# Rotary embedding in a two-layer diffusion backbone: the rotated half taken by transfers within SBUF instead of a TensorE product

## The reference, cut to what matters

```python
def apply_rope(x, cos, sin):
    q = HEAD_DIM // 4                      # 16 of the 64 rows of a head
    x0, x1, x2, x3 = x[..., :q], x[..., q:2 * q], x[..., 2 * q:3 * q], x[..., 3 * q:]
    rot = jnp.concatenate([-x1, x0, -x3, x2], axis=-1)
    return x * cos + rot * sin
```

## Time and profile before

| | |
|---|---|
| median of 3 runs | 1598.11 us (1596.82 to 1600.96) |
| the profiled execution, its own time | 1596.81 us |
| its span | 1594.7 us |
| PE busy, DVE busy | 1553.0 us (97%), 789.8 us (50%) |
| granted TensorE clock | 0.998 over the span |
| line 1970, rotation products | 28 records: two for each of 14 tiles |
| weights, SP line 532 | 180 transfers of 512 KB, median 3.5 us to landing |

### The profile page before, as it was taken

The page is one execution under the profiler, slowest core; times in us unless marked ns, Lnnn a source line. Parts: engine busy times, 40 slices in busy tenths (PEclk is TensorE's granted clock), DMA queues, the critical chain, the costliest instruction groups (busy, mean ns, idle before and its releaser), DMA issues.

```text
span 1594.7 us, 25334 instructions
## 1 busy us (share of the span) xinstructions
PE 1553.0 (97%) x10785; PEld 1290.1 (81%) x10785; DVE 789.8 (50%) x1276; ACT 550.1 (34%) x725; POOL 541.4 (34%) x244
## 2 busy tenths in 40 slices
PE   6999999899999999999999999999999999999998
PEld 3888754478888888888888888855479998998997
DVE  5897786678466534333234333666534221221324
ACT  5744335464322112221122234255544322222233
POOL 0040046413323332332233223256643444444442
PEclk9999999999999999999999999999999999999999
DMA  9532100052233333333433222200022222223223
GB/s 376 209 119 67 54 28 0 3 205 101 93 132 132 110 129 133 119 119 139 150 110 131 66 69 73 72 14 1 1 67 93 93 93 93 93 93 106 94 93 106
DMA packets 44607, 158.55 MB, mean 99 GB/s; under 512 B 4784, under 2 KB 8240, under 8 KB 42960
## 3 DMA queue, kind: packets, MB, share of 16 engines
q1 hardware_dynamic: 44064, 156.74, 28.1%
q0 software_dynamic: 432, 0.20, 0.1%
HBM read 154.95 MB, written 2.10 MB: 98 GB/s over the span
## 4 chain that ended last, share of the span: by engine, by line
PE 75%; DVE 2%; ACT 1%; issue 1%; POOL 1%; DVEq 0%; POOLq 0%
PE psum L1850 67%; PE psum L2099 2%; PE psum L1927 1%; PE psum L2067 1%; DVE osb L1379 1%; PE psum L1998 1%; PE psum L1895 1%; POOL acc L622 1%; PE psum L2115 0%; DVE mx L1275 0%; PE psum L2084 0%; PE psum L2073 0%; PE psum L2071 0%; PE psum L2069 0%; PE psum L1970 0%
## 5 line engine op out<-in xcount | busy, mean ns | idle before, releaser
L1850 PE MATMUL psum<-act,whi 128*128 128x258 f32 (+2 forms) x3968 | 784.5, 318 | 0.0
L649 POOL TENSOR_TENSOR wlo<-raw,whi 128x1024 fp32r<-128x1024 f32 (+1 forms) x162 | 390.4, 2410 | 791.2 <-ACT whi L683 791.2
L1850 PEld LDWEIGHTS psum<-act,whi 128*128 128x128 f32 x3968 | 588.1, 189 | 57.3 <-issue 3.7
L1850 PE MATMUL psum<-act,wlo 128*128 128x512 f32 (+1 forms) x1984 | 472.1, 316 | 0.0
L1850 PEld LDWEIGHTS psum<-act,wlo 128*128 128x128 f32 x1984 | 309.0, 189 | 26.7
L683 ACT ACTIVATE whi<-raw 128x1024 fp32r<-128x1024 f32 (+1 forms) x180 | 187.1, 1040 | 336.2 <-DMA raw<-weights_dram 336.1
L1176 DVE SCALAR_TENSOR_TENSOR tmps<-psum,rs 128x256 f32<-128x256 f32 (+1 forms) x176 | 78.2, 486 | 349.1 <-PE psum L1850 345.6
L1128 DVE SCALAR_TENSOR_TENSOR product<-adr,cb 128x1024 f32<-128x1024 f32 x128 | 177.6, 1418 | 5.9 <-ACT cb L750 3.0
L1619 DVE SCALAR_TENSOR_TENSOR xT<-psum,mod,xT 128x512 f32<-128x512 f32 x93 | 58.3, 655 | 223.6 <-PE psum L1850 223.6
L1850 PE MATMUL psum<-gh,whi 128*128 128x512 f32 x507 | 152.6, 357 | 0.0
L1850 PE MATMUL psum<-gh,wlo 128*128 128x512 f32 x507 | 152.5, 358 | 0.0
(11 more groups left out here) (205 smaller groups left out, 1313.0 us busy)
## 6 DMA issues: line engine op xcount, KB each, us to landing
raw<-weights_dram SPq DMA_DIRECT2D x180, 512.0 KB, 3.5
adr<-adat_dram SPq DMA_DIRECT2D x80, 512.0 KB, 4.7
ada_w<-ada_dram SPq DMA_DIRECT2D x8, 1024.0 KB, 14.3
xT<-x_in_dram SPq DMA_DIRECT2D x3, 1024.0 KB, 16.9
xT<-x_in_dram SPq DMA_DIRECT2D x2, 1536.0 KB, 8.0
cb<-crow_dram SPq DMA_DIRECT2D x2, 1024.0 KB, 10.6
out_dram<-fin SPq DMA_DIRECT2D x8, 256.0 KB, 2.3
stage<-weights_dram SPq DMA_DIRECT2D x1, 512.0 KB, 9.4
```

The costliest lines, as they stand in the source:

```text
L649: nc.gpsimd.tensor_tensor(wlo[:, s, 0:w], raw[:, s, 0:w], whi[:, s, 0:w].bitcast(F32), ALU.subtract).then_inc(sem("s_lo"), 1)
L1850: last = MM(out_[:, o:o + t1 - t0], w_, a_[:, t0:t1], start=k == order[0] and j == 0, stop=k == order[-1] and j == 2)
```

## The change: what it does

`rotated` and its matrix `rot` are gone from PE's program, with the waits on `a_nrm`, `a_rsin` and layer 1's `s_tile` that stood beside it. In its place SP issues eight transfers for each of the 14 tiles (`turn`): 16 partitions of 512 f32 (32 KB) each, from the head tile into `ropet`, quarter q taken from quarter q XOR 1. `ropet` is then multiplied by the sine in place. The negation moves into the table of the sine. SP waits for `a_nrm` (layer 0) or `s_tile` (layer 1), and for an earlier `a_rope`, so that the buffer is free. DVE waits for all eight transfers of a tile. In DVE's program only layer 1's last block changes its order.

```diff
+        TURNED = {11: (0, 0), 13: (0, 1), 14: (0, 2), 16: (0, 3), 17: (0, 4)}
+        TURNED.update({FIRST[("proj", 1)] + (j + 2 if j else 1): (1, j) for j in range(9)})
...
+        def turned(L, j):
+            return sem(f"a_rot{j % 2}"), 16 * 8 * (j // 2 + 1 + L * (3 - j % 2))
...
+            def turn(L, j):
+                if L == 0:
+                    sp.wait_ge(sem("a_nrm"), j + 1)
+                    if j >= 1:
+                        sp.wait_ge(sem("a_rope"), j)
+                else:
+                    sp.wait_ge(sem("s_tile"), 19 + (j + 2 if j else 1))
+                    if j >= 2:
+                        sp.wait_ge(*na("rope", 1, j - 1))
+                src_, dst_ = prep_tiles(L)[j][0], rope_place(L, j)
+                for q in range(8):
+                    a, b = 16 * q, 16 * (q ^ 1)
+                    sp.dma_start(dst_[a:a + 16, :], src_[b:b + 16, 0:NX]).then_inc(turned(L, j)[0], 16)
...
+                if n - RING + 1 in TURNED:
+                    turn(*TURNED[n - RING + 1])
...
             def roped_sine(L, j):
-                dve.wait_ge(*na("rot", L, j + 1))
-                if L == 0 and j >= 1:
-                    dve.wait_ge(sem("a_rope"), j)
-                TT(ropet[L][:, j % 2 * L, 0:NX], rot_out(L, j), sin, ALU.mult).then_inc(sem("a_rsin"), 1)
+                dve.wait_ge(*turned(L, j))
+                TT(rope_place(L, j), rope_place(L, j), sin, ALU.mult).then_inc(sem("a_rsin"), 1)
...
                     if b["m"] == 9:
-                        roped_sine(1, 7)
                         maxima(1, 1, 4)
-                        roped_sine(1, 8)
                         top(1, 1)
-                        roped(1, 7, sine=False)
-                        roped(1, 8, sine=False)
+                        roped(1, 7)
+                        roped(1, 8)
...
-            def rotated(L, j):
-                if L == 0:
-                    pe.wait_ge(sem("a_nrm"), j + 1)
-                elif j >= 2:
-                    pe.wait_ge(*na("rsin", L, j - 1))
-                MM(rot_out(L, j), rot, prep_tiles(L)[j][0][:, 0:NX], start=True, stop=True) \
-                    .then_inc(sem("a_rot"), 1)
...
-    con[:, CC_SIN:CC_SIN + NX] = np.tile(np.sin(ang), (2, 1))
+    con[:, CC_SIN:CC_SIN + NX] = np.tile(np.sin(ang), (2, 1)) * np.where(np.arange(P) % (2 * quarter) < quarter, -1.0, 1.0)[:, None]
...
-    con[:, CC_ROT:CC_ROT + P] = np.kron(np.eye(2), r)
```

More of the change, by code:

```diff
@@ L75 @@
 CC_BLK = CC_ONES + P
-CC_ROT = CC_BLK + P
-CC_MF = CC_ROT + P
+CC_MF = CC_BLK + P
 CC_MB = CC_MF + CH
@@ L344, in build @@
         blk = con[:, CC_BLK:CC_BLK + P]
-        rot = con[:, CC_ROT:CC_ROT + P]
         cos = con[:, CC_COS:CC_COS + NX]
@@ L363, in build @@
         names += [f"s_{n}" for n in ("sq", "sqadd", "nps", "rs", "nhh", "nhl")]
-        names += [f"a_{n}" for n in ("sq", "ms", "rs", "nrm", "rot", "rsin", "rcos", "rope", "khi", "klo", "zone", "vps",
+        names += [f"a_{n}" for n in ("sq", "ms", "rs", "nrm", "rot0", "rot1", "rsin", "rcos", "rope", "khi", "klo", "zone", "vps",
                                      "vtok", "qhi", "qlo", "M", "mx", "top", "R", "neg", "e", "S", "exp", "add", "pv", "sum",
@@ L391, in build @@
         ALL = {"m": sum(len(u["pieces"]) for u in U[0]), "t": sum(len(u["steps"]) for u in U[0])}
-        ONCE = {"rot": 5, "rsin": 5, "rcos": 5, "rope": 5, "khi": 1, "klo": 1, "vps": 1, "vtok": 1, "qhi": 4, "qlo": 4,
+        ONCE = {"rsin": 5, "rcos": 5, "rope": 5, "khi": 1, "klo": 1, "vps": 1, "vtok": 1, "qhi": 4, "qlo": 4,
                 "M": ALL["m"], "mx": ALL["m"], "S": ALL["t"], "exp": ALL["t"], "pv": ALL["t"],
@@ L462, in prep_tiles, with rope_place @@
                 [(ksrc(1), None)] + [(bigs[1][:, 2 + t, :], None) for t in range(8)]
[L464 to L468, removed]
+        def rope_place(L, j):
+            return ropet[L][:, j % 2 * L, 0:NX]
+        def turned(L, j):
+            return sem(f"a_rot{j % 2}"), 16 * 8 * (j // 2 + 1 + L * (3 - j % 2))
         def vT_out(L):
@@ L1226, in roped_sine, with roped @@
             def roped_sine(L, j):
-                dve.wait_ge(*na("rot", L, j + 1))
-                if L == 0 and j >= 1:
-                    dve.wait_ge(sem("a_rope"), j)
-                TT(ropet[L][:, j % 2 * L, 0:NX], rot_out(L, j), sin, ALU.mult).then_inc(sem("a_rsin"), 1)
-            def roped(L, j, sine=True):
+                dve.wait_ge(*turned(L, j))
+                TT(rope_place(L, j), rope_place(L, j), sin, ALU.mult).then_inc(sem("a_rsin"), 1)
+            def roped(L, j):
                 t = prep_tiles(L)[j][0][:, 0:NX]
-                rs_ = ropet[L][:, j % 2 * L, 0:NX]
-                if sine:
-                    roped_sine(L, j)
+                rs_ = rope_place(L, j)
+                roped_sine(L, j)
                 TT(t, t, cos, ALU.mult).then_inc(sem("a_rcos"), 1)
@@ L2058, in scores @@
                         pe.wait_ge(*na("exp", L, t - 1))
-                    if t == 1:
-                        pe.wait_ge(*(na("mx", 0, 7) if L == 0 else na("rsin", 1, 9)))
+                    if t == 1 and L == 0:
+                        pe.wait_ge(*na("mx", 0, 7))
                     keys, qs = slice(kt * P, kt * P + P), slice(q0 + qa, q0 + qb)
@@ L2220, in behind_block @@
                     pe.wait_ge(sem("g_kcpA"), 1)
-                    rotated(0, 0)
                 if n == 12:
@@ L2224, in behind_block @@
                     means(1)
-                    pe.wait_ge(sem("a_rsin"), 1)
                     linear_keys(2)
@@ L2228, in behind_block @@
                     pe.wait_ge(sem("a_rs"), 2)
-                    rotated(0, 1)
                     pe.wait_ge(sem("g_kcpD"), 2)
@@ L2235, in behind_block @@
                     pe.wait_ge(sem("a_rs"), 3)
-                    rotated(0, 2)
                 if n == 15:
@@ L2239, in behind_block @@
                     means(3)
-                    pe.wait_ge(sem("a_rsin"), 3)
                 if n == 16:
                     pe.wait_ge(sem("a_rs"), 4)
-                    rotated(0, 3)
                     pe.wait_ge(*na("mx", 0, 2))
@@ L2249, in behind_block @@
                     rows(0, 0)
-                    rotated(0, 4)
                 if pieces_within(n, 8):
@@ L2265, in within_block @@
                 if n == 14:
-                    pe.wait_ge(sem("a_rsin"), 2)
                     updates(0)
@@ L2270, in within_block @@
                     updates(2)
-                if n == 17:
-                    pe.wait_ge(sem("a_rsin"), 4)
             def gla(sums):
@@ L2368, in _ @@
                         maxima(1, 1, 4)
-                    for m in ready_tiles(b["m"]):
-                        pe.wait_ge(sem("s_tile"), 19 + m + 1)
-                        if m == 1:
-                            values_turned(1)
-                        else:
-                            rotated(1, max(m - 1, 0))
+                    if b["m"] == 2:
+                        pe.wait_ge(sem("s_tile"), 19 + 2)
+                        values_turned(1)
             last_blocks()
@@ L2393, in _shape_constants @@
     con[:, CC_BLK:CC_BLK + P] = np.kron(np.eye(2), np.ones((64, 64))) / 64.0
-    r = np.zeros((64, 64), np.float32)
-    for j in range(quarter):
-        r[quarter + j, j] = -1.0
-        r[j, quarter + j] = 1.0
-        r[3 * quarter + j, 2 * quarter + j] = -1.0
-        r[2 * quarter + j, 3 * quarter + j] = 1.0
-    con[:, CC_ROT:CC_ROT + P] = np.kron(np.eye(2), r)
     j, i = np.arange(CH)[:, None], np.arange(CH)[None, :]
```

## The result

| | before | after |
|---|---|---|
| median of 4 runs each, us | 1598.44 (1596.82 to 1600.96) | 1611.58 (1611.11 to 1612.16) |
| ratio, 95% interval | | 1.0082 [1.0067, 1.0097] |
| span of the profiled execution, us | 1594.7 | 1609.0 |

The changed kernel is 13.1 us slower. The forecast was 1599.6 us with a range from 1594 to 1604.5, so both missed, and so did the likeliest sign, "no change".

The account below looks back on a forecast made before the run. PE, busy 97% of the span, was taken to set the pace nearly everywhere. Layer 0's +3.2 and layer 1's -1.7 gave +1.5 us on a median of 1598.1: 1599.6 us, range 1594 to 1604.5.

Parts of the forecast that it names:

- no change: Whole kernel: a result within about 0.3%, 4.8 us, which a measurement cannot tell apart; chance 0.73.
- everything behind is later by 215.35 - 212.10 = 3.2 us: Layer 0, block 18: piece (1, 4) starts at 215.35 instead of 212.10, so layer 0 ends 3.2 us later.
- some 7 us: Layer 0, block 18: PE stands this long before piece (1, 4), held by DVE's maximum of piece (1, 3).
- L: Way from a finished tile to a landed turn: eight serial SP issues plus one landing, 5.5 us.
- 2L - 7.75: Layer 0's general loss in us at piece (1, 4), for L above 4.
- Late by 0.55 us: Layer 1: the turn of m = 3 lands 0.55 us after DVE wants it for the sine.
- I take 1 us: Layer 1's attention: cost of tile 8's sine, cosine and sum running beside POOL's sums, delaying PE's next piece.
- The formula: Layer 0 at piece (1, 4): loss 2L - 7.75 for L above 4; below 4, L - 3.75, a gain.
- Rival B: Slow turns, each landing like a weight block: L = 6.9, layer 0 loses 6.0 us, 1604 us; chance 0.19.
- Rival A: The eight transfers overlap and behave as one: L = 2.7 us, -4.3 us in all, 1593.8 us; chance 0.13.
- before attention: Layer 1's end: PE wins 1.8 us, but ACT's table load limits the lead to 2.7; net term -1.0 us.
- If that cover went: Layer 0: block 20's load leaves about 3 us later, costed at nothing; uncovered, part of the same 3 us.

Follow-up runs that it names:

- e5: Changed kernel plus products nobody reads, keeping PE busy in its waits in block 18 (layer 0) and block 5 (layer 1); 1608.33 us.
- e4: Changed kernel with turns in layer 1 alone, layer 0's products put back on PE; 1600.87 us.
- e6: Changed kernel with DVE reordered in both layers, the product with the sine moved later, behind pieces of maxima; 1595.44 us.
- e2: Changed kernel with one transfer of 128 partitions a tile instead of eight of 16, swapping nothing (timing only); 1595.19 us.
- e1: Changed kernel with four transfers of 32 partitions a tile instead of eight of 16, swapping halves of a head (timing only); 1597.17 us.
- e3: Changed kernel with turns in layer 0 alone, layer 1's products put back on PE; 1604.43 us.
- e8: As e6, with four of each turn's eight transfers issued by ACT instead of SP; 1598.80 us.
- e9: e4 with layer 1's DVE order of e6, layer 0 as before the change; 1590.81 us.

## Why the prediction was wrong

The sum came out at +1.5 us and the spans differ by 14.3. The 12.8 us between them are one term that the sum does not have and three that are too small:

- **The failed step is "everything behind is later by 215.35 - 212.10 = 3.2 us", after a wait of "some 7 us": there is no term for the clock.** The sum foresaw the long wait and took PE's work behind it at full speed. Behind the three waits of 6.66, 3.59 and 3.08 us PE ran at half clock for 6.8, 6.8 and 3.4 us, which costs 5.7 us by the table (1.5, 2.8 and 1.4). e5 shows for the first two that it is the waits' doing. This is the largest miss. Without this and without the two misses in layer 1 below, a right L alone would have added 1.8 + 0.9 us and left the time at 1602.3 us, inside the range.
- **L, "8 x 0.40 + 2.3 = 5.5 us", measured 6.35.** Its issue term was mis-sized: 0.37 to 0.43 us were read from issues that stand alone, while eight in a row take 0.59 us each and a pitch of 0.616. The landing counts from the issue's start, so one issue drops out, and is 2.0. The errors partly cancel. L is still inside the prediction's own limits (wrong if under 4.5 or over 6.5), but as the loss is 2L - 7.75, it makes +5.0 of +3.2 us. The profile of before had better rows, where SP issues one transfer right behind another at the start of the program:

```profile
0.75 0.40 SPq L540 DMA_DIRECT2D par<-params_dram  x1
1.21 0.42 SPq L541 DMA_DIRECT2D con<-consts_dram  x1
...
3.64 1.27 SPq L532 DMA_DIRECT2D raw<-weights_dram  x2
```

Their pitch is 0.46 us and, for the two weight loads, 0.63. From these L = 8 x 0.63 + 1.1 to 2.3 could have been the upper bound, and a follower behind a turn shows it again: the weight load at 196.93 takes 0.58 us, where the median of its line is 0.33.
- **"Late by 0.55 us" in block 5 was 3.0 us.** 0.9 us of it come from L. The other 1.6 are the landing of the turn's last transfer, 3.6 us and not 2.0. SP issues a 512 KB weight load at 1006.77 right behind it, but that does not explain it: the turn from 995.42 on has such a load right behind it as well, at 1000.40, and landed on time:

```profile
L548 SPq DMA_DIRECT2D ropet<-big x8: 512/589/590, 995.4 to 999.8; - x8
...
DMA to landing us min/median/max: 1.9/2.0/2.0
```

So did the turn ahead of the load at 196.93 (1.9 us), and in the turn of tile 2, from 164.58 on, transfers took up to 3.4 us with no weight load issued until 170.88. In e4, e5 and e6 the last transfer of the same turn is slow again, 3.2 to 3.3 us, and so is e2's single one, 3.7 us, with no weight load right behind. The cause stays open, and no run varied it.
- **The last turn, "I take 1 us", cost 3.7.** The place and the cause (DVE beside POOL's sums) were right, as far as the timelines tell: sine and sum took 1.60 and 2.27 us where 0.69 is usual. The prediction had the landing nearly where it came, but no term for DVE's wait of 2.60 us ahead of it.
- **The formula and its place were right**: DVE stands 2.26 and 5.20 us before the sine (predicted 1.5 and over 4), PE 6.66 us at piece (1, 4) (predicted some 7). The changed kernel confirms the upper branch of the formula, e1 and e2 the lower. Rival B had L and the slower side nearly right (6.9) for the wrong reason, a landing like a weight block's each time, and still only 1604 us. Rival A is refuted: the eight are issued one after the other.
- **Right:** PE really gains 0.86 us per product behind m = 1 and 3 (-1.8 for -1.7); the five in blocks with maxima give nothing, since PE waits for DVE's maximum there by 0.6 to 1.2 us (the row at 1024.10); before attention -1.5 was measured for -1.0.
- **"If that cover went"**: block 20's load behind the turn was named and rightly cost nothing in this kernel, but became one of the bounds in e6.

On dispatch, the Trainium skill ("DMA: Bandwidth & Descriptors", section "Anatomy of one DMA — SWDGE (gpsimd) path") has some 50 ns for GpSimd's path; SP's 0.59 us here are twelve times that, so the figure does not carry over to SP. Its fixed 2.0 us a transfer agree with the median landing of 2.0 us measured here.

## What to carry to other kernels

An instruction taken from the busiest engine pays only where no other engine comes last right behind it; what replaces it needs a place in the consumer's order that is late by its whole latency, so move the consumer along with it (16 us lay between the same instructions in two orders). Price a chain of small transfers by issue pitch times their number, and prefer a few with many partitions where the permutation allows it. A wait on TensorE can cost again in granted clock, as each one of 2.0 us or more did here, so look at the stretch behind each new wait and give it a term of its own.

## What the runs showed of the hardware

- SP's issue of a transfer within SBUF: 0.51 us for the first strip of a turn and 0.59 for the followers, of 16 or 32 partitions alike; 0.47 for a single one of all 128, though it moves the most bytes.
- Landing from the issue's start: 2.0 us in the median for 32 and for 64 KB, 2.3 for 256 KB, and up to 3.6 in some turns (3.7 in e2). A weight load right behind did not decide it (1.9 to 2.0 us ahead of the loads at 196.93 and 1000.40, 3.6 ahead of that at 1006.77).
- Half clock at PE's waits: 6.8 us at waits of 6.66 and 3.59 us, 6.67 (e3) and 3.53 (e8); 3.4 us at 3.08 us, 3.67 (e1), 3.15 (e4), 2.26 (e8), 2.07 (e2) and 2.00 (e6); none behind 0.68 us at piece (1, 4) of e6. In the 13 profiles, behind their first 20 us, no wait of PE of 2 us or more is without such a stretch, and the kernel before has no wait that long. The length of the wait alone does not decide between 3.4 and 6.8. Where PE does small jobs with many short waits, between 305 and 330 us, it was 3.4, 6.8 and 13.7 us in three kernels with the same layer 0 (before, e9, e4).
- Issued from ACT, four such transfers occupy ACT for 2.71 us.
- DVE beside POOL: the same 128x512 sum took 0.69 us in e4, begun before POOL's sum, and 2.27 at 1062.58, begun 0.1 us after it; in e6 a 128x512 product of another line took 2.82 beside POOL's remainder of the weights (`wlo`).
